# A new opening for a one-core mLSTM and S5 layer: key block in the first chunks, compact scan parameters, early sample states, 22 products of the ones tile

## What is computed

```python
h = rmsnorm(x, g_mix)
proj = h @ w_in + b_in            # q, k, v, o (4 heads of 256), ig, fg, u (512), gl
lf = log_sigmoid(fg)
hA, C, n, m = mlstm_mixer(q, k * DH ** -0.5, v, ig, lf, C0, n0, m0)
# exact causal attention form: running sum of lf, running max, exp weights, k^T v state
yA = (sigmoid(o) * headnorm(hA)) @ w_a
yS, sr, si = s5_mixer(u, ...)     # abar = exp(dt * A), diagonal complex scan, Re(C s) + D u
yB = glu(gelu(yS)) @ w_b
x = x + (sigmoid(gA) * yA + sigmoid(gB) * yB) @ w_out
x = x + (silu(hf @ w_ff1) * (hf @ w_ff3)) @ w_ff2     # hf = rmsnorm(x, g_ffn)
y = rmsnorm(x, g_fin)
```

## Time and profile before

| | us |
|---|---|
| three runs | 1030.63, 1031.87, 1032.90 |
| median | 1031.87 |
| the profiled execution | 1032.94 |
| its span in the trace | 1031.0 |
| PE busy | 976.4 |
| DVE, ACT, POOL busy | 567.1, 419.8, 189.1 |

### The profile page before, as it was taken

The page is one execution under the profiler, slowest core; times in us unless marked ns, Lnnn a source line. Parts: engine busy times, 40 slices in busy tenths (PEclk is TensorE's granted clock), DMA queues, the critical chain, the costliest instruction groups (busy, mean ns, idle before and its releaser), DMA issues.

```text
span 1031.0 us, 19911 instructions
## 1 busy us (share of the span) xinstructions
PE 976.4 (95%) x8196; PEld 933.5 (91%) x8196; DVE 567.1 (55%) x936; ACT 419.8 (41%) x625; POOL 189.1 (18%) x346
## 2 busy tenths in 40 slices
PE   4896989999999999889999999999999999999994
PEld 3895779899889989789999999999999999999994
DVE  6799586388358449475333465544445444432334
ACT  5422726743672492552323344333333333222221
POOL 3197852454184103100000000000000000000000
PEclk9998999999999999899999999999999999999997
DMA  6232416227323423334243322323232323233312
GB/s 257 65 103 75 175 42 255 77 74 253 100 94 128 171 103 132 113 123 172 96 123 103 103 82 82 103 82 101 81 102 81 101 82 99 84 103 102 102 41 83
DMA packets 27172, 114.67 MB, mean 111 GB/s; under 512 B 3332, under 2 KB 3380, under 8 KB 25192
## 3 DMA queue, kind: packets, MB, share of 16 engines
q1 hardware_dynamic: 21744, 79.21, 24.1%
q0 software_dynamic: 2992, 25.43, 6.5%
q10 hardware_dynamic: 2376, 9.17, 2.3%
HBM read 100.40 MB, written 13.40 MB: 110 GB/s over the span
## 4 chain that ended last, share of the span: by engine, by line
PE 90%; DVE 7%; ACT 1%; issue 1%; DMA 1%; DVEq 0%; SPq 0%; ACTq 0%
PE G L1414 69%; PE G L1488 4%; PE Q L1414 2%; PE Q L1495 2%; PE Q L1536 2%; PE G L1576 1%; PE Q L1523 1%; PE Q L1533 1%; PE G L1567 1%; PE Q L1499 1%; DVE c_samples L1195 1%; PE Q L1625 1%; PE G L1568 1%; PE Q L1452 1%; PE Q L1596 1%
## 5 line engine op out<-in xcount | busy, mean ns | idle before, releaser
L411 ACT ACTIVATE w_high<-raw 128x1024 fp32r<-128x1024 f32 (+1 forms) x147 | 155.4, 1058 | 351.1 <-PE G L1414 309.3
L1414 PE MATMUL G<-h_high,w_high 128*128 128x256 f32 x1360 | 278.1, 286 | 13.7 <-DVE v_samples L1149 9.1
L936 DVE TENSOR_TENSOR w_low<-raw,w_high 128x1024 fp32r<-128x1024 f32 x146 | 181.2, 1241 | 178.0 <-ACT w_high L411 177.2
L1414 PE MATMUL G<-h_low,w_high 128*128 128x256 f32 x1360 | 275.5, 284 | 0.0
L1414 PE MATMUL G<-h_high,w_low 128*128 128x256 f32 x1360 | 275.4, 284 | 0.0
L1414 PEld LDWEIGHTS G<-h_high,w_high 128*128 128x128 f32 x1360 | 212.6, 190 | 16.3 <-DVE v_samples L1149 9.3
L1414 PEld LDWEIGHTS G<-h_low,w_high 128*128 128x128 f32 x1360 | 212.7, 190 | 0.0
L1414 PEld LDWEIGHTS G<-h_high,w_low 128*128 128x128 f32 x1360 | 212.3, 190 | 0.0
L1414 PE MATMUL G<-hidden_high,w_low 128*128 128x256 f32 x352 | 70.9, 282 | 0.0
L1414 PE MATMUL G<-hidden_low,w_high 128*128 128x256 f32 x352 | 70.8, 282 | 0.0
L1414 PE MATMUL G<-hidden_high,w_high 128*128 128x256 f32 x352 | 70.6, 282 | 0.0
(11 more groups left out here) (368 smaller groups left out, 1567.6 us busy)
## 6 DMA issues: line engine op xcount, KB each, us to landing
raw<-wst SPq DMA_DIRECT2D x147, 512.0 KB, 3.5
c_samples<-c POOLq DMA_DIRECT2D x4, 2048.0 KB, 9.0
out_cs<-c_samples POOLq DMA_DIRECT2D x4, 2048.0 KB, 7.5
v_spread<-v_scratch ACTq DMA_DIRECT2D x4, 1024.0 KB, 4.7
x_tokens<-xt SPq DMA_DIRECT2D x4, 520.0 KB, 6.0
x_residual<-xt POOLq DMA_DIRECT2D x1, 2080.0 KB, 8.4
out_y<-x_residual ACTq DMA_DIRECT2D x8, 260.0 KB, 2.2
small<-small ACTq DMA_DIRECT2D x1, 1785.0 KB, 8.6
```

The source lines that it names most:

```text
L411: return act.activation(out, in_, ACT.Copy, **kw)
L936: tt(WL[n.slot()][:], raw[n.slot()][:], WH[n.slot()][:].bitcast(F32), ALU.subtract).then_inc(w_lo, 1)
L1414: last = mm(o, w[slot][:, c], h[:, k, c0_:c0_ + width], start=start and x == 0 and t == 0, stop=stop and x == n - 1 and t == 2)
```

## The change

1. PE: eight products of `ones` with itself (128 x 128) into an unused bank ahead of the sums of squares, and 14 behind them. Their result is not read.
2. PE: unit 2 (first key) is done chunk by chunk with unit 1 in the first half; in the second half its high part follows unit 1. Unit 4 goes to another PSUM pair, unit 5 to the banks of unit 2. The wait for `rows_in` moves from unit 4 to the values.
3. ACT: the exp of `dt` stands behind the second square instead of the fourth; a dummy root ahead of the sums loads the table; the 1.8 MB load `small` is issued behind the roots; the high half of unit 2 ahead of the chunks; the two sines between the halves.
4. DVE: the last `h_low` of the first half ahead of the second reciprocal; powers and low halves of units 3 and 4 ahead of the gate rows; the scan parameters shorter (24 instructions for the six squarings, and 24 for the layout of all levels and heads) and placed **before** the running sum.
5. POOL loads `CS` for head 0 as soon as the tokens are no longer read; ACT scales it in front of unit 8's sigmoid.
6. Addresses: the gate rows use five buffers in another place, so that `CS` may be written early.

The core of the diff (the squarings and layout are new code in place of `put` per level):

```diff
-            ig, fg, ab, lf, cum, on4, mx = gt[0], gt[1], gt[2], gt[5], gt[6], gt[7], gt[8]
+            ig, fg, ab, lf, cum, mx = gt[0], gt[1], gt[2], gt[3], gt[4], gt[1]
...
 # ACT
-                if k == 3:
+                if k == 1:
                     act.wait_ge(par_in, 16)
                     act.activation(par[:, 2, :], par[:, 2, :], ACT.Exp).then_inc(s5_dt, 1)
-                if k == 6:
-                    act.dma_start(sm[:], small[:, 0:NSM]).then_inc(sm_in, 16)
...
+            act.activation(junk_a[:], eps[:], ACT.Sqrt)
...
+            act.dma_start(sm[:], small[:, 0:NSM]).then_inc(sm_in, 16)
             high(At(1))
+            high(At(2))
...
-                if h >= 1:
+                if h == 0:
+                    scale_cs()
+                else:
                     gelu(h - 1)
...
 # POOL
             load_vb(0)
+            guard(xg_ready, 2 * KC)
+            load_cs(0)
             pool.wait_ge(uq_clear, 1)
...
 # DVE
                 if i == KC:
-                    low(At(2))
+                    h_low(i - 1)
                     invert(1)
+                    low(At(2))
...
             k_or_q(0, 1)
+            pre, pim = a_pow[:, 0, 2, 256:272], a_pow[:, 1, 2, 256:272]
+            for lev in range(LEVELS):
+                qre, qim = tp[0][:, 16 * lev:16 * lev + 16], tp[1][:, 16 * lev:16 * lev + 16]
+                own.add(tt(tp[0][:, 128:144], pre, pre, ALU.mult))
+                own.add(tt(tp[1][:, 128:144], pim, pim, ALU.mult))
+                own.do(stt(qim, pre, 2.0, pim, ALU.mult, ALU.mult))
+                own.do(tt(qre, tp[0][:, 128:144], tp[1][:, 128:144], ALU.subtract))
+                pre, pim = qre, qim
...
+            put("one_re", "one_im", 1, a_pow[:, 0, 0, 256:272], a_pow[:, 1, 0, 256:272])
+            put("scan_re", "scan_im", LEVELS, tp[0][:, 0:16 * LEVELS], tp[1][:, 0:16 * LEVELS])
             dve.wait_ge(fln, 1)
...
 # PE
+            pe.wait_ge(consts, 1)
+            for _ in range(8):
+                mm(G[:, A, 0:P], ones[:], ones[:], start=True, stop=True)
...
+            for _ in range(14):
+                mm(G[:, A, 0:P], ones[:], ones[:], start=True, stop=True)
...
-                pe.wait_ge(q0_ready, h + 1)
+                if h == 0:
+                    pe.wait_ge(rows_in, 1)
```

More of the change, by code:

```diff
@@ L448, in _ @@
                     copy(HH[:, k, c0_:c0_ + w], xg[k % 2][:, c0_:c0_ + w]).then_inc(hh_ready, 1)
[L449 to L454, removed]
+                if half == 0:
+                    act.wait_ge(s5_ang, 1)
+                    act.activation(tp[4][:], tp[1][:], ACT.Sin).then_inc(s5_trig, 1)
+                    act.activation(tp[5][:], tp[3][:], ACT.Sin, bias=half_pi[:, 0:1], scale=-1.0).then_inc(s5_trig, 1)
             after(At(0))
@@ L1020, in _ @@
-            own.settle()
-            stt(ab[:], fg[:], -1.0, fg[:], ALU.mult, ALU.max).then_inc(rows_in, 1)
-            own.add(dve.memset(on4[:], 1.0))
-            own.do(ts(lf[:], fg[:], 0.0, None, ALU.min))
-            low(At(N_MIX + RING))
             def take_u(h):
@@ L1052, in k_or_q, with tsc @@
                 low(n.plus(1 + j + RING))
-            k_or_q(0, 0)
+            own.add(dve.memset(ones[:], 1.0))
+            dve.memset(half_pi[:], 1.5707963267948966)
+            dve.memset(eps[:], EPS).then_inc(consts, 1)
+            dve.memset(UQ[:], 0.0).then_inc(uq_clear, 1)
+            def tsc(o, a, s1, op1, s2=None, op2=ALU.bypass):
+                own.do(ts(o, a, s1, s2, op1, op2) if s2 is not None else ts(o, a, s1, None, op1))
+            ai, dt = par[:, 1, :], par[:, 2, :]
+            t = [x[:] for x in tp]
@@ new lines, in _, with invert, h_low @@
+            tt(gate_cols(WL[0][:]), gate_cols(raw[0][:]), gate_cols(WH[0][:].bitcast(F32)), ALU.subtract).then_inc(w_lo, 1)
+            def invert(half):
+                c0_, w = HALVES[half]
+                dve.wait_ge(rx_root, half + 1)
+                own.do(dve.reciprocal(rx[:, c0_:c0_ + w], rx[:, c0_:c0_ + w]))
+            def h_low(i):
+                k, (c0_, w) = i % KC, HALVES[i // KC]
+                dve.wait_ge(hh_ready, i + 1)
+                tt(HL[:, k, c0_:c0_ + w], xg[k % 2][:, c0_:c0_ + w], HH[:, k, c0_:c0_ + w].bitcast(F32), ALU.subtract).then_inc(hl_ready, 1)
@@ new lines, in _ @@
+            invert(0)
+            dve.wait_ge(gb_in, 16)
+            for i in range(2 * KC):
+                k, (c0_, w) = i % KC, HALVES[i // KC]
+                if i == 5:
+                    low(At(1))
+                if i == KC:
+                    h_low(i - 1)
+                    invert(1)
+                    low(At(2))
+                if i >= 2:
+                    dve.wait_ge(hl_ready, i - 1)
+                stt(xg[k % 2][:, c0_:c0_ + w], X[:, k, c0_:c0_ + w], g_mix[:, k:k + 1], rx[:, c0_:c0_ + w], ALU.mult, ALU.mult).then_inc(xg_ready, 1)
+                if i not in (0, KC):
+                    h_low(i - 1)
@@ new lines, in put @@
+            def put(name_re, name_im, levels, re, im):
+                re, im = (x.rearrange("p (l t j) -> p t l j", l=levels, j=PAIRS) for x in (re, im))
+                to_im = hpv(name_im).rearrange("p h (l c j) -> p h l c j", c=2, j=PAIRS)
+                for h in range(H):
+                    own.add(dve.tensor_copy(par_of(h, name_re).rearrange("p (l j) -> p l j", j=PAIRS), re[:, h]))
+                    own.add(ts(to_im[:, h, :, 0, :], im[:, h], -1.0, None, ALU.mult))
+                    own.add(dve.tensor_copy(to_im[:, h, :, 1, :], im[:, h]))
```

179 lines of the change are left out of this document (72 added, 107 removed).

## The result

| | before | after |
|---|---|---|
| median of the runs measured together, us | 1032.38 | 1025.90 |
| lowest to highest | 1030.63 to 1033.87 | 1025.39 to 1027.60 |
| ratio, 95% interval | | 0.9944 [0.9925, 0.9963] |
| the profiled execution, its span | 1032.94, 1031.0 | 1025.75, 1023.8 |

The change makes the kernel faster by 5.8 us by the ratio (3.8 to 7.7 by its interval, 6.5 by the medians). The forecast was 11.1 us: the direction holds, the size is about half.

A forecast was written before the change was run, and what follows sets the result against it. The PE, busy 976.4 of 1031.0 us, was taken as the bound, with only its waits and slow stretches to win. 5.3 us by unit 8 plus 5.8 from the sample states made 11.1: 1020.8 us, range 1014 to 1026.5.

The forecast's parts named there:

- The bound and its release: PE's idle waits: 9.1 us before unit 8, 2.9 before unit 12, 1.1 before sample queries; new wait of 11.5 at values.
- Opening: Start of the kernel up to DVE's copy into head_params: 1.9 us earlier, from 38.57 to 36.7 us.
- The 22 products at nothing: PE's ones products around the sums of squares: may delay PE a few us, costed at nothing, covered by the values' wait.
- The scan parameters: DVE's 48 small instructions before the running sum: 8.5 us, the middle of the bounds 5.5 and 11.4.
- rival C: Scan parameters on DVE: each of 24 squarings waits for a POOL product; block 25.4 us, time 1037.7; chance 0.03.
- the 5.3 us: Gain at the end of unit 8: it begins 2.5 us earlier and runs 2.8 us shorter at full clock.
- The clock term: Values on the PE: the new wait in front of them lowers the clock, costing 2.4 us.
- The sample states: Sample queries and unit 12: early load and scaling remove waits of 1.1 and 2.9 us and 1.8 of slow clock; 5.8 us.
- A: Rival at the values: DVE isn't last there, its list to the bias limits next; 4.8 us more gain, 1016.0; chance 0.10.
- B: Rival in head 0: ACT reaches unit 9's sigmoid late and the state product waits; up to 5.0 us, 1025.8; chance 0.08.
- my case: Main forecast for the whole kernel: 11.1 us gained, 1020.8 us, within 1016.4 to 1025.1; chance 0.76.
- D: Rival for the whole kernel: opening's gain lost at the values, sample states wait on something else; about 1031; chance 0.03.

The follow-up runs named there:

- Experiment 1: The changed kernel without the 22 products of the ones tile, nothing else changed; 1026.01 us, ratio 0.9944.
- experiment 3: The changed kernel with the low half of unit 7 moved right behind that of unit 6, ahead of the scan parameters; 1020.27 us, ratio 0.9902.
- experiment 2: The changed kernel with POOL held before pack_c and form_f until DVE finishes the 48 scan-parameter instructions; 1024.47 us, ratio 0.993.
- table of four: Gains against the kernel before: block in new place, samples late 1.1 us, early 5.8; block back behind bbar, samples late 5.2, early 9.8.
- experiment 5: The changed kernel with the 48 scan-parameter instructions moved back behind the last product for bbar; 1021.67 us, ratio 0.9905.
- experiment 4: The changed kernel with the sample states loaded and scaled as in the kernel before; 1031.03 us, ratio 0.9989.

## Why the prediction was right or wrong

**The bound and its release: right.** The waits named were what the change removed, and the new wait stood where it was put, in front of the values with `w_low` as releaser. That its length, 14.3 us, lies in the 8 to 15 given is luck: the PE was free at 59.5 us, not at 57.9, and counted from 57.9 the wait would have been 15.9.

**Opening: right in its sum, not in every term.** The copy into `head_params` stands at 37.29 us (36.7 forecast), a gain of 1.3 us where 1.9 was taken. The sums of squares gave none of it: they end at 17.33 us, where they ended at 16.78 before. Behind the copy `rows_in` is given at 50.4 (50.1), the low half of unit 6 starts at 53.97 and the block at 55.35, where 55.1 and 56.3 were forecast. Only `rows_in` is 0.3 us late; at the block the sum was 1 us on the safe side.

**The 22 products at nothing: right in size, wrong in cover.** The prediction let the wait at the values cover them. Experiment 1 shows that this wait is 14.3 us with and without them, and that the PE's wait for the first chunk takes them up. Of the faster clock that they were to give, the first chunks had it in the changed kernel. The sums of squares did not: their first four passes took 2.10 us, as without the products. In five other runs with the products they took 1.14 or 1.15 us (in experiment 3 at a granted clock of 1.00, which was at 0.50 from 9 us on), and there the copy came at 36.4 to 36.8 us, against 36.9 to 37.5 in the others. Whether that is worth something in the time is open; experiment 1 shows no difference.

**The scan parameters: this term failed.** The prediction took 8.5 us, the middle between 5.5 and 11.4, and gave 6 to 11 as the sign of being right; it was 14.35. The lower bound held (5.37 us in experiment 2). The upper bound was no bound: it was the old block's 11.4 us, measured beside other products of POOL, and I took it over to a place beside `form_f` and `form_bbar`. The words "the same neighbour", by which rival C was set aside, were wrong too: the old block stood beside POOL's tables. Here DVE gets through two squarings or four layout instructions per POOL product, the stalled one included, so the price of the place is the number of POOL's products in it times their length. The block put back takes 10.8 us, in the new place 14.35, on the same 48 instructions.

Two consequences follow. The values began 4.4 us later than forecast (73.8 against 69.4), and unit 8 4.0 us later (96.0 against 92.0), which is the whole of what is missing from the 5.3 us: 5.3 less 4.0 is about the 1.4 measured at its end. And the move itself, which the sum did not price apart from the rest, is a loss of some 4 us (table of four). With the block left in its place the opening brings 5.2 and the samples 4.6.

**The clock term: right in kind.** 2.4 us was taken for the slow start of the values. They took 16.45 us; at 5.78 / 48 for each of 120 it would be 14.45, so it was 2.0. Unit 8 ran in 5.77 as forecast.

**The sample states: right.** 5.8 us was forecast, 5.7 stands in the chain at the end of unit 12, and 4.6 to 4.7 are measured by the times. It held with less room than forecast: DVE's 16 products took 11.96 us instead of 7.23 and ended 6.2 us before the PE's sample queries, not some 10, and `s_out` was done 0.9 us before the PE asked for it.

**The rivals.** A (DVE not last, 1016.0) did not come, but experiment 3 makes it nearly true by one line, and 1020.3 is what it gave. B (ACT the bound) is excluded: ACT's sigmoid behind unit 9 waited 1.07 us for the PE (1.91 before), and the PE's wait for its result is 1.0 us, as before. C (slower) had the mechanism and the place, and the size wrong: it let each of the 24 squarings wait for one product, 25.4 us; it was every second of them and four of the layout instructions, 14.35, below the 19.6 at which it would have turned. A part of C's price came due, and the term of my case (5.5 to 11.4) left no room for it. The Trainium skill, SBUF — State Buffer, "Who interferes with whom", says that whoever issues first gets the shared ports for its whole instruction and the other is blocked. I set this aside because the old block stalled seldom; the trace of the changed kernel agrees with the page, within 0.04 us at the stalls shown, and what varies is how often it is met. D (nothing) fell.

**The order of DVE's row.** The prediction took the low half of unit 7 behind block and running sum as given and summed along it. It did not ask what experiment 3 asks, whether the instruction that the PE waits for has to stand there.

## What to carry to other kernels

In this kernel a block of small DVE instructions had no duration of its own while POOL multiplied beside it (the same 48 took 10.8 and 14.35 us in two places, and 5.37 with POOL held): count POOL's products in that stretch, and let DVE pass one to three instructions between two stalls. So a duration read in one place bounds nothing in another; move such a block only after asking who works beside the new place. When a block moves to the front of an in-order queue, first move ahead of it the one instruction that another engine waits for. That is worth it as far as the next wait: with V 10 us earlier the kernel won about 1 us more, since the masked weights came next. And parts of a change should be priced and measured singly: here two gains of about 5 us hid a loss of 4.

## What the runs showed of the hardware

- Also copies and scalings of one tensor stall beside POOL, not only products of two: in experiment 5 a scaling and a copy of 4 columns took 1.24 and 1.23 us beside two POOL products of 1.32, and in experiment 2, with POOL held, all of them took 0.16 to 0.17.
- Larger DVE instructions seem to pay alike. The 16 updates of the sample states (128 x 256) took 11.96 us beside a POOL that was busy for 10.7 of 12.0 us, and 7.23 in the kernel before, where POOL was busy for 2.3 of 7.2. In the late place again they took 7.35 us (experiment 4, POOL busy for 2.4). No run held POOL back there, so that POOL is the cause is not shown.
- TensorE's clock was at the higher of its levels (1.2 and 2.4 GHz) in the first chunks when the PE was kept busy ahead of them: a pass of the `ones` products took 0.24 us in the first eight (16 in 3.78 us) and 0.12 in the last fourteen (28 in 3.29 us), and the chunks followed at 1.00. Without the products the first chunks ran at a granted clock of 0.50, and the time was the same.
